# Reading the experts' first matrix in groups of 2048 columns, with the gate rows kept in other memory

## The reference

```python
def _swiglu(h, w_gate_up, w_down):          # w_gate_up (1024, 7168), w_down (3584, 1024)
    gu = h @ w_gate_up
    g, u = gu[..., :D_FF], gu[..., D_FF:]   # D_FF = 3584
    return (jax.nn.silu(g) * u) @ w_down

def _moe(h, router, w_gate_up, w_down):
    top_v, top_i = lax.top_k((h @ router).astype(jnp.float32), 2)
    gates = jax.nn.softmax(top_v, axis=-1)
    ...
    for e in range(8):
        y = y + gate_full[..., e:e + 1] * _swiglu(h, w_gate_up[e], w_down[e])
```

## Time and profile before

| | |
|---|---|
| three runs, median (lowest, highest) | 1521.85 us (1520.17, 1522.1) |
| the profiled execution | 1522.17 us |
| its span, first to last instruction | 1520.2 us |
| TensorE busy | 1481.3 us (97%) |
| VectorE busy | 1158.3 us (76%) |
| ScalarE busy | 991.1 us (65%) |
| bytes read from HBM | 459.55 MB |

### The profile page before, as it was taken

How to read it: one execution, slowest core, us unless ns; L and a number is a source line. 1 busy time by engine, 2 the same in 40 slices (tenths; PEclk the granted TensorE clock), 3 DMA queues, 4 the chain that set the end, 5 groups by cost and what they waited for, 6 DMA issues and landing times.

```text
span 1520.2 us, 19543 instructions
## 1 busy us (share of the span) xinstructions
PE 1481.3 (97%) x7678; PEld 1208.7 (80%) x7678; DVE 1158.3 (76%) x1021; ACT 991.1 (65%) x869; POOL 132.2 (9%) x137
## 2 busy tenths in 40 slices
PE   8999999999989999999999999999999999999996
PEld 6888888899969987888777788777888777888774
DVE  5555445454565456899899988899898999898997
ACT  5544434343453337777798777888776888776986
POOL 0000000006034314000000200000100000000000
PEclk9999999999999999999999999999999999999999
DMA  9655555567516653899999999999999999999996
GB/s 333 214 170 190 168 192 171 189 192 224 194 57 213 206 185 126 329 356 355 366 405 417 398 407 405 395 408 415 399 408 403 395 408 415 399 404 408 393 391 220
DMA packets 151056, 468.26 MB, mean 308 GB/s; under 512 B 9856, under 2 KB 15872, under 8 KB 138416
## 3 DMA queue, kind: packets, MB, share of 16 engines
q1 hardware_dynamic: 144784, 453.93, 79.8%
q0 software_dynamic: 2816, 9.96, 2.3%
q10 hardware_dynamic: 3360, 3.06, 0.7%
HBM read 459.55 MB, written 7.37 MB: 307 GB/s over the span
## 4 chain that ended last, share of the span: by engine, by line
PE 79%; DVE 13%; ACT 3%; DMA 1%; SPq 1%; issue 1%; DVEq 0%; ACTq 0%
DVE wlo L418 9%; PE bS L437 6%; PE bS L438 6%; PE bS L436 6%; PE bY L436 6%; PE bY L438 6%; PE bY L437 6%; PE bG L436 4%; PE bG L438 4%; PE bU L436 4%; PE bG L437 4%; PE bU L438 4%; PE bU L437 4%; DVE wlo_more L418 2%; ACT whi L412 2%
## 5 line engine op out<-in xcount | busy, mean ns | idle before, releaser
L418 DVE TENSOR_TENSOR wlo<-raw,whi 128x2048 fp32r<-128x2048 f32 x364 | 827.2, 2296 | 179.6 <-ACT whi L412 178.4
L412 ACT ACTIVATE whi<-raw 128x2048 fp32r<-128x2048 f32 x364 | 692.3, 1915 | 262.1 <-PE bS L438 118.2
L418 DVE TENSOR_TENSOR wlo_more<-raw_more,whi 128x2048 fp32r<-128x2048 f32 x60 | 136.4, 2288 | 10.7 <-ACT whi L412 10.6
L412 ACT ACTIVATE whi<-raw_more 128x2048 fp32r<-128x2048 f32 x60 | 114.5, 1914 | 28.0 <-DMA raw_more<-in_m_w_gate_up_dram 8.4
L1086 PE MATMUL bY<-whi,hTh 128*128 128x512 f32 x224 | 91.5, 408 | 6.9 <-DVE wlo L418 4.9
L436 PE MATMUL bY<-whi,hTh 128*128 128x512 f32 x224 | 89.8, 401 | 0.0
L437 PE MATMUL bY<-whi,hTl 128*128 128x512 f32 x224 | 89.1, 398 | 0.0
L437 PE MATMUL bS<-whi,eTl 128*128 128x512 f32 x192 | 76.4, 398 | 0.0
L436 PE MATMUL bS<-whi,eTh 128*128 128x512 f32 x192 | 76.4, 398 | 0.0
L1086 PE MATMUL bS<-whi,eTh 128*128 128x512 f32 x192 | 76.3, 398 | 0.0
L1087 PE MATMUL bY<-wlo,hTh 128*128 128x512 f32 x184 | 73.2, 398 | 0.0
(11 more groups left out here) (536 smaller groups left out, 3336.4 us busy)
## 6 DMA issues: line engine op xcount, KB each, us to landing
raw<-in_m_w_gate_up_dram SPq DMA_DIRECT2D x184, 1024.0 KB, 14.5
raw<-in_m_w_down_dram SPq DMA_DIRECT2D x90, 1024.0 KB, 14.4
raw_more<-in_m_w_gate_up_dram SPq DMA_DIRECT2D x40, 1024.0 KB, 14.6
raw<-in_b_w_in_dram SPq DMA_DIRECT2D x36, 1024.0 KB, 5.1
raw<-in_f_w_gate_up_dram SPq DMA_DIRECT2D x28, 1024.0 KB, 5.2
raw_more<-in_m_w_down_dram SPq DMA_DIRECT2D x20, 1024.0 KB, 14.2
raw<-in_f_w_down_dram SPq DMA_DIRECT2D x14, 1024.0 KB, 5.0
raw<-in_a_w_out_dram SPq DMA_DIRECT2D x4, 1024.0 KB, 16.8
```

Source lines behind the costliest of these rows:

```text
L412: nc.scalar.activation(whi[:, h], raw_of(r), ACT.Copy).then_inc(hi_done, 1)
L418: nc.vector.tensor_tensor(wlo_of(r), raw_of(r), whi[:, h].bitcast(F32), ALU.subtract).then_inc(lo_done, 1)
```

## The change

The first matrix, as one array of 7168 columns, is read in three groups (`GROUPS`) of 2048 columns, eight tiles each, and a rest of 1024 columns in four tiles (from `NARROW` = 24 on). A tile of a group is 128 rows of the matrix by 2048 columns: each partition gets 8192 contiguous bytes, where it got two pieces of 4096. The rest's tiles have pieces of 4096 bytes, where they had 2048. The second matrix is read as before.

The groups cross the border between gate and up. Group 0 holds gate slabs 0 to 3, group 1 gate slabs 4 to 6 and up slab 0, group 2 up slabs 1 to 4, the rest up slabs 5 and 6 (`UPS_OF`). Each group fills the four banks G, S0, S1, U at once, and the next group's first tile needs them emptied (`bank_free`). All seven gate slabs are made before most up sums exist, so they wait in a new tile `parked`, which lies over `hTl` (same size; a slab's gate rows lie where its `hTl` comes later). The turns move back: after tiles 17, 24, 25, 27, 29, 31 and 33, and in item 7 after 17 and then 24 to 29. A new semaphore `gu_psum` tells that a bank other than the last is complete.

The core of the diff (the half item's parts on VectorE and ScalarE, and TensorE's, are alike in form):

```diff
-PAIRS = SLABS // 2
-SINGLE = 8 * PAIRS
+GROUPS = 2 * FF // 2048
+NARROW = KD * GROUPS
+UPS_OF = ((), (0,), (1, 2, 3, 4), (5, 6))
...
+        parked = place("parked", [SLABS, 512], F32)
...
-        gate_rows = lambda j: (mbuf, mbuf_odd)[j % 2][:, 0]
-        up_rows = lambda j: (mbuf, mbuf_odd)[j % 2][:, 1]
+        gate_rows = lambda j: parked[:, j]
+        up_rows = lambda j: (mbuf, mbuf_odd)[j % 4 // 2][:, j % 2]
...
-            if t < SINGLE:
-                g, r = divmod(t, 8)
-                part, q = divmod(r, 4)
-                c = part * FF + g * 1024
-                return gate_up[q * 256:q * 256 + 256, c:c + 1024].rearrange("(k p) n -> p k n", p=P)
+            if t < NARROW:
+                g, kb = divmod(t, KD)
+                return gate_up[kb * P:kb * P + P, g * 2048:g * 2048 + 2048]
             if t < DOWN:
-                part, kh = divmod(t - SINGLE, 2)
-                c = part * FF + PAIRS * 1024
-                return gate_up[kh * 512:kh * 512 + 512, c:c + 512].rearrange("(k p) n -> p k n", p=P)
+                q = t - NARROW
+                return gate_up[q * 256:q * 256 + 256, GROUPS * 2048:2 * FF].rearrange("(k p) n -> p k n", p=P)
...
+        gate_up_banks = G, S0, S1, U
+        def column_sums(engine, n, g, s):
+            if s == (3 if g < GROUPS else 1):
+                engine.wait_ge(tile_used, count(n, FFN_TILES, T_MOE + (KD * g + KD if g < GROUPS else DOWN)))
+            else:
+                engine.wait_ge(gu_psum, count(n, 10, 3 * g + s + 1))
...
             def half_item(n, k, amid=lambda g: None, late=lambda: None, by_half=False, before_down=lambda: None):
+                def bank_free(g, s):
+                    if g == 1:
+                        pe.wait_ge(gate_copied, count(k, SLABS, s + 1))
+                    if g == 2 and s < 3:
+                        pe.wait_ge(gate_copied, count(k, SLABS, s + 5))
+                    if g == 2 and s == 3:
+                        pe.wait_ge(up_copied, count(k, SLABS, 1))
+                    if g == 3:
+                        pe.wait_ge(up_copied, count(k, SLABS, s + 2))
...
+                turns = {17: 0, 24: 1, 25: 2, 27: 3, 29: 4, 31: 5, 33: 6}
+                if by_half:
+                    turns = {17: 0, 24: 1, 25: 2, 26: 3, 27: 4, 28: 5, 29: 6}
+                for t in range(DOWN):
+                    gate_up_product(t)
+                    if t in turns:
+                        turn(turns[t])
...
+                for t in range(FFN_TILES):
+                    ahead(t)
+                    if t in (7, 15):
+                        for j in range(4) if t == 7 else range(4, SLABS):
+                            copy_gate(j)
+                    if t in (15, 23, 27):
+                        copy_ups((t - 7) // KD if t < 27 else 3)
...
+                    if t in (14, 22, 27):
+                        muls({14: 1, 22: 2, 27: 3}[t])
```

More of the change, by code:

```diff
@@ L1039, in turn @@
                     mm.then_inc(ht_psum, 1)
[L1041 to L1052, removed]
@@ new lines, in full_item @@
+                for t in range(DOWN):
+                    gate_up_product(t)
+                    if t in turns:
+                        turn(turns[t])
+                    if t in (3, 11, 25):
+                        amid(t // KD)
+                before_down()
+                for t in range(DOWN, FFN_TILES):
+                    pe.wait_ge(ht_lo, count(k, SLABS, PAIRS0 + (t - DOWN) // 2 + 1))
+                    down_product(t)
+                    if t in turns:
+                        turn(turns[t])
+                    if t == DOWN + 5:
@@ new lines, in gate_up_product @@
+                def gate_up_product(t):
+                    tile_ready(T_MOE + t, n)
+                    for s, blk, kb, stop in blocks_of(t, False):
+                        if t < KD:
+                            tokens_ready(n, kb, s)
+                        if kb == 0:
+                            bank_free(t // KD, s)
+                        w = wblk_backward(T_MOE + t, blk, n)
+                        pe.matmul(backward(gate_up_banks[s], 0, 512), eTh[:, kb], w[0], start=kb == 0, stop=False)
+                        mm = pe.matmul(backward(gate_up_banks[s], 0, 512), eTh[:, kb], w[1], start=False, stop=stop)
+                        if stop and s < (3 if t < NARROW else 1):
+                            mm.then_inc(gu_psum, 1)
+                    mm.then_inc(tile_used, 1)
@@ L1085, in product @@
                         w = wblk_backward(T_MOE + t, blk, n)
[L1086 to L1087 removed]
+                        pe.matmul(backward((Y0, Y1)[s], 0, 512), hTh[:, kb], w[0], start=kb == 0, stop=False)
+                        mm = pe.matmul(backward((Y0, Y1)[s], 0, 512), hTh[:, kb], w[1], start=False, stop=stop)
                     mm.then_inc(tile_used, 1)
@@ L1552, in half_item @@
-                ahead(DOWN + 4, DOWN + 5)
-                if not by_half:
-                    slab_hi(SLABS - 1)
-                ahead(DOWN + 6)
-                if by_half:
-                    y_cut(0)
-                else:
-                    late()
-                ahead(*range(DOWN + 7, DOWN + 12))
-                if by_half:
-                    late()
-                ahead(DOWN + 12, DOWN + 13)
+                turned = {18: 0, 25: 1, 26: 2, 28: 3, 30: 4, 32: 5, 34: 6}
+                if by_half:
+                    turned = {18: 0, 25: 1, 26: 2, 27: 3, 28: 4, 29: 5, 30: 6}
@@ new lines, in half_item @@
+                for t in range(FFN_TILES):
+                    ahead(t)
+                    if t == 3:
+                        amid(0)
+                    if t in (7, 15):
+                        for j in range(4) if t == 7 else range(4, SLABS):
+                            copy_gate(j)
+                    if t in (15, 23, 27):
+                        copy_ups((t - 7) // KD if t < 27 else 3)
+                    if t in turned:
+                        slab_silu(turned[t])
+                    if t - 1 in turned:
+                        slab_hi(turned[t - 1])
+                    if t == DOWN + 6:
+                        y_cut(0) if by_half else late()
+                    if by_half and t == DOWN + 11:
+                        late()
```

273 lines of the change are left out of this document (94 added, 179 removed).

## The result

The changed kernel takes 1529.81 us (median of five runs, 1526.54 to 1530.01), the kernel before beside it 1522.1 us (median of five). The ratio is 1.0046, with a 95% interval of 1.0035 to 1.0057: slower, by about 7 us. The forecast was 1520.2 us and its range ended at 1528.

The account below looks back on a forecast made before the run. TensorE was taken to bound full items, VectorE half items, with loads reaching only item 7. Terms 3 x 0.0 + 0 - 1.7 on 1522.17 us gave 1520.5, and 1520.2 us with the median 0.3 lower; range 1514 to 1528.

Parts of the forecast that it names:

- Full items: Items 0, 2, 4, 6: same matmuls and turns, each loss hidden by three tiles in hand; 0, bound +0.5 us an item.
- 2.4 for this: Item 7: VectorE's wait for ScalarE shrinks from 5.6 to at best item 3's 3.2 us, a gain of 2.4.
- 1.6 for old stops: Item 7: ordinary stops like item 3's, beyond the 1.6 us at its start, go with the old order; 1.6 us gained.
- ScalarE's runs of four copies: Half items 1, 3, 5: copies out of the banks don't stop VectorE; TensorE waits about 0.1 us a group.
- Item 7's net gain of 1.7 us: Item 7: 2.4 from load waits plus 1.6 from old stops, less 2.3 for a new stop, makes 1.7 us gained.
- 2.3 for the turns: Item 7: six turns in tiles 24 to 29 make TensorE lag, so VectorE stops for about 2.3 us.
- Its waits for loads should go altogether.: Item 7: its loads begin some 15 us earlier and lose about 8 us over its length, so no load waits remain.
- the sum's +0.4: Half items 1, 3, 5: TensorE's waits for copies out of the banks, about 0.1 us a group, add 0.4 us an item.
- -1.6 for old stops: Half items 1, 3, 5: the old order's stops go, 1.6 us an item gained.
- +1.2 for the turns in tiles 24 to 33: Half items: TensorE falls 3.7 us behind VectorE there; 2.5 are covered, 1.2 us stop VectorE.
- The sign that it named: Profile after, half items: VectorE waits 2 us for ScalarE around tiles 30 to 34 and hardly before.
- The first rival: Turns crowd TensorE in tiles 24 to 33: half items end 2.2 us later, item 7 gains nothing, 1528 us; chance 0.22.

Follow-up runs that it names:

- the loads alone: The kernel before, same instructions and order, with only the changed kernel's piece sizes for the first matrix's loads: 1518.7 us, ratio 0.9977.
- the spare matmuls: The changed kernel with twelve matmuls of 512 columns into an unused bank just before tile 24 of item 7: 1526.25 us, ratio 1.0026.
- the earlier copies: The changed kernel with ScalarE's four up-sum copies of group 2 before whi of tile 26, in half items: 1521.9 us, ratio 0.9998.
- the run with few turns: The changed kernel with the up-sum copies before whi of tile 26 and 4 of 16 small matmuls in each of item 7's turns: 1519.98 us, ratio 0.9987.
- the run of the order alone: The changed kernel with each first-matrix tile loaded by two DMAs, in pieces of 4096 and 2048 bytes as before: 1532.07 us, ratio 1.0059.

## Why the prediction was wrong, step by step

**Right.** Full items hold at 122.5. Loads set no item but the last: in items 1 to 6 ScalarE waited for them 45 times before, 31.8 us in all, and never after, and none of these items became shorter. The queue lost the 32,768 packets. Taken by themselves, the loads give 3.3 us in item 7, where the forecast had 2.4 for this, and its 1.6 for old stops on top.

**The step that failed** is the one on ScalarE's runs of four copies: "So VectorE doesn't stop, and TensorE waits about 0.1 us a group." It asked for whom the copies push back `whi` of tile t+4, and found nobody, which is true. It compared the copies' spacing (0.48 us) with the banks' (0.47), and so took the run to begin when the first bank is complete. It names `whi` of tile t+3 in front of the run, but gives no time to it, and this copy is itself late by what ScalarE lags at that point of the item. At the ends of the first two groups that does no harm: TensorE waits 0.4 us for bank G, the tile takes 2.55 us and the next one 1.87, together as long as two of VectorE's 2.20. At the third group's end the lag is such that bank G is free 0.96 us after TensorE asks in a half item, and 2.73 us in item 7. Sized 0.1 at this group, it measured 0.9 us in each of three items (100.78 against 99.91 with the copies moved by one place, in item 3). For item 7 the sum had no such term at all, and there it measured 6.4 us with the clock behind it (107.11 against 100.70).

**Item 7's net gain of 1.7 us** was a loss of 5.3. From the 98.5 us of the loads alone to 107.1 there are 8.6 us: 4.2 of half clock (the spare matmuls), 2.2 more that the earlier copies take back (6.4 in all), and 2.2 that the new order of the turns costs. The forecast had 2.3 for the turns, less 1.6 for old stops, so 0.7 for this part. Without the copies its 1.7 would have stood against 1.2 (101.85 - 100.70), which is close partly by luck: the loads gave 0.9 more than it had and the turns took 1.5 more. The clock was in no term and in no rival. It should have been a question at once, since the change gave TensorE a new dependency in the one item where loads run late.

**"Its waits for loads should go altogether."** For down tiles they did. With the new loads alone the waits for gate-up tiles in item 7 had gone as well; the new order brought two of them back. Until tile 24 item 7 now has one turn where it had four, and TensorE passes these tiles sooner. From the item's first matmul to the end of tile 23 it is now 1462.41 - 1409.51 = 52.9 us, 2.20 us a tile. Before, it was 55.6 us, 2.32 a tile: the item began at 1406.75 and tile 23's last matmul at 1461.98, as the kernel before's timeline has it:

```profile
1406.75 0.40 PE L1086 MATMUL bG<-whi,eTh 128*128 128x512 f32 x1
...
1461.98 0.40 PE L1087 MATMUL bS<-wlo_more,eTh 128*128 128x512 f32 x1
1462.37 0.48 PE L1086 MATMUL bG<-whi,eTh 128*128 128x512 f32 x1
```

The two late copies of a tile begin 2.56 us apart (1460.04 to 1462.60), which is the loads' pace for 4096-byte pieces in the earlier trace rows, and TensorE takes a tile every 2.2, so the lead is used up just when the copies stand behind `whi`. The two late tiles, 0.51 and 0.64 us, were worth only 1.1 us; what they hit made them expensive.

**Half items.** Apart from the copies (the sum's +0.4, four groups at 0.1), the forecast had -1.6 for old stops and +1.2 for the turns in tiles 24 to 33. These two can't be told apart, but their sum can: with the copies moved the items are 99.9 against 100.0, so -0.1 stands against the forecast's -0.4. The sign that it named is there too: from 1024 to 1050, in item 3, VectorE waits 1.9 us for ScalarE, where it was 0.8. The first rival (turns crowd TensorE, 2.2 us an item, 1528) lies nearest in time by chance, and its mechanism was wrong: item 3 is 100.8 long, not 102.

**Sum.** Forecast -1.7; measured 3 x 0.8 + 3 x 0.1 + 5.3 = 8.0, the span's 8.0.

## What to carry to other kernels

When copies out of PSUM banks are gathered into a run, ask for each bank when it is complete, what stands ahead of its copy on that engine, and when TensorE asks for the bank again; here a copy one place too late stopped TensorE, while a tile's preparation one place later was covered by the tiles in hand. A stop of a few microseconds is priced with the clock that it may cost: here 2.7 us of waiting brought another 4.2. Longer pieces for loads paid only in the item where late loads reached TensorE, so find that stretch first and leave the order of the rest alone.

## What the runs showed of the hardware that was not expected

- One stop of TensorE of 2.7 us was followed by 10.2 us at 1.2 GHz (1464.4 to 1474.6), with matmuls of 512 columns 0.43 us apart instead of 0.23. The same came behind a stop of 2.7 us in the run with few turns (0.57 from 1470 to 1474), and behind one of 1.9 us within a stretch of 8 us with 5.99 busy in the run of the order alone (0.79 from 1448 to 1456). Stops of 0.96 us in the half items, and of 1.3 us in two half items of that run, were followed by none. Twelve useless matmuls in the stop kept the clock, for a gain of 4.2 us in item 7.
- Pieces of 8192 bytes instead of 4096 in 24 tiles of an item, and of 4096 instead of 2048 in four, were worth 0.23% of the whole kernel (0.9977 [0.9967, 0.9987]). Of the items only the last one became shorter, by 3.3 us. By the 512 bytes that the Trainium skill's page "DMA: Bandwidth & Descriptors", section "Specifications", gives for line rate, they would have been worth nothing; the measurement decides against it.
